# Modulation on TensorE, more work put beside choosing, more row buffers, and top sums sought among 70 pairs

## The reference, cut to what matters

```python
s_top, i_top = lax.top_k(scores, 16)            # twice 16 of 128, for two halves of a query
cand = s_top[:, :, 0, :, None] + s_top[:, :, 1, None, :]      # 16 x 16 sums
best, pos = lax.top_k(cand.reshape(..., 256), 16)
idx = i_top0[pos // 16] * 128 + i_top1[pos % 16]              # one of 16384 experts
gate = softmax(best)
h = gelu(sum_d u[idx, d] * x[d])
out = sum_k gate_k * h_k * v[idx_k]
```

```python
mod = silu(c) @ w_ada + b_ada      # 1024 x 6144; shift, scale and gate, twice each
h = rms_norm(x, g_mix) * (1.0 + scale1) + shift1
```

## Time and profile before

| | us |
|---|---|
| median of 3 runs | 3753.48 (3752.86 to 3761.49) |
| the profiled execution | 3752.87 |
| its span in the trace | 3750.8 |
| layer 1, first choice to first second product | 735.9 to 1542.5 |
| layer 2, the same | 2525.9 to 3215 |

### The profile page before, as it was taken

One profiled execution on the slowest core, in us unless ns is written; L12 is line 12 of the kernel. 1 busy time (PEld: TensorE's weight loads), 2 busy tenths in 40 slices (PEclk: granted clock), 3 DMA queues, 4 the chain that ended last, 5 costly groups with the idle time before them and its releaser, 6 DMA issues.

```text
span 3750.8 us, 46474 instructions
## 1 busy us (share of the span) xinstructions
PE 3396.3 (91%) x18582; PEld 2973.6 (79%) x18582; DVE 2809.2 (75%) x4525; ACT 1410.3 (38%) x1889; POOL 1151.4 (31%) x726
## 2 busy tenths in 40 slices
PE   6999998977777889999999899788888999999998
PEld 5978578877776879878888776778888999888887
DVE  3356543399888999578888586548999998688887
ACT  4324532232222556333333344423322566333333
POOL 0000000058788873233333000000433333233332
PEclk9999998988888999999999899889999999999999
DMA  3212133257777989999998320124777999999996
GB/s 124 79 35 68 45 103 100 79 187 249 244 249 249 305 296 363 340 341 357 362 357 330 93 68 6 68 74 140 255 249 240 311 366 354 356 361 357 363 362 238
DMA packets 373498, 855.56 MB, mean 228 GB/s; under 512 B 22449, under 2 KB 237329, under 8 KB 340130
## 3 DMA queue, kind: packets, MB, share of 16 engines
q1 hardware_dynamic: 299554, 584.12, 44.6%
q0 software_dynamic: 73728, 268.47, 20.0%
HBM read 746.58 MB, written 105.93 MB: 227 GB/s over the span
## 4 chain that ended last, share of the span: by engine, by line
PE 61%; DVE 29%; DMA 4%; ACT 3%; issue 2%; POOL 2%; SPq 0%; DVEq 0%; POOLq 0%; ACTq 0%
PE ps L294 31%; PE ps L1404 27%; DVE parts L277 6%; DVE scr L1609 5%; DMA scr<-in_p_rows_u,cst 3%; DVE scr L1652 2%; DVE scr L1586 2%; DVE scr L1590 1%; DVE scr L1584 1%; PE ps L316 1%; DVE scr L1588 1%; DVE scr L1558 1%; DVE scr L1644 1%; DVE scr L1552 1%; DVE scr L1582 1%
## 5 line engine op out<-in xcount | busy, mean ns | idle before, releaser
L294 PE MATMUL ps<-ht_hi,parts 128*128 128x384 f32 (+1 forms) x5008 | 1423.3, 360 | 98.0 <-DVE parts L277 93.7
L294 PEld LDWEIGHTS ps<-ht_hi,parts 128*128 128x128 f32 x5008 | 961.3, 197 | 158.4 <-DVE parts L277 105.3
L277 DVE TENSOR_TENSOR parts<-ring,parts 128x2048 fp32r<-128x2048 f32 (+1 forms) x317 | 740.8, 2337 | 322.8 <-ACT parts L269 322.6
L269 ACT ACTIVATE parts<-ring 128x2048 fp32r<-128x2048 f32 (+1 forms) x317 | 606.5, 1913 | 822.9 <-PE ps L1404 675.7
L294 PE MATMUL ps<-ht_lo,parts 128*128 128x384 f32 (+1 forms) x2504 | 892.5, 356 | 0.0
L322 ACT ACTIVATE scr<-ps 128x384 f32<-128x384 f32 (+3 forms) x496 | 244.1, 505 | 1131.9 <-PE ps L294 1071.5
L1737 POOL DMA_INDIRECT scr<-in_p_rows_u,cst x256 | 439.5, 1717 | 658.0 <-DVE scr L1609 471.1
L1737 POOL DMA_INDIRECT scr<-in_peer_v,cst x256 | 381.9, 1492 | 702.8 <-DVE xres L1626 609.0
L1404 PE MATMUL ps<-parts,ht_lo 128*128 128x512 f32 x2304 | 528.9, 390 | 7.2 <-DVE ht_lo L1699 7.2
L1404 PE MATMUL ps<-parts,ht_hi 128*128 128x512 f32 x2304 | 529.3, 390 | 4.5 <-DVE ht_hi L1699 4.5
L1404 PEld LDWEIGHTS ps<-parts,ht_lo 128*128 128x128 f32 x2304 | 433.6, 188 | 97.5 <-DVE ht_lo L1699 7.6
(11 more groups left out here) (227 smaller groups left out, 3013.4 us busy)
## 6 DMA issues: line engine op xcount, KB each, us to landing
ring<-in_peer_u SPq DMA_DIRECT2D x128, 1024.0 KB, 6.7
ring<-in_peer_v SPq DMA_DIRECT2D x128, 1024.0 KB, 7.6
hbuf<-scr SPq DMA_DIRECT2D x128, 384.0 KB, 7.6
gbuf<-scr SPq DMA_DIRECT2D x96, 512.0 KB, 8.9
scr<-gbuf SPq DMA_DIRECT2D x64, 768.0 KB, 9.4
scr<-hbuf SPq DMA_DIRECT2D x64, 768.0 KB, 12.1
ring<-in_w_in SPq DMA_DIRECT2D x35, 1024.0 KB, 5.3
scr<-in_w_ada SPq DMA_DIRECT2D x48, 512.0 KB, 7.6
```

What stands on the lines that cost most here:

```text
L269: e.activation(halves(m)[0], slot_view(m)[:, 0:units[m][0]], ACT.Copy).then_inc(A.sem, A.up(("hi", m)))
L277: e.tensor_tensor(lo, slot_view(m)[:, 0:units[m][0]], hi.bitcast(F32), ALU.subtract).then_inc(V.sem, V.up(("lo", m), ("slot", m)))
L294: ins = e.matmul(ps, l, r, start=(i == 0), stop=(i == n - 1))
```

## The change

1. `w_ada` is taken as TensorE's stationary operand: for each of 48 steps, 8 products of [128x128] float32 weights with one column of `silu(c)`, into column `n` of one PSUM bank that is held for all 48. One addition of the bias ([128, 48]), one transpose, one copy by ScalarE and one store follow at `n` = 48, 50 and 52. POOL has no part in it any more, and the 48 closing additions, bias loads and stores are gone. Load `n + 1` of `w_ada` is issued at step `n`.
2. `peer_order` gets other costs and two rates. Now 87 half units and 92 dots stand before the first spread step (13 half units in block 0, then 24, 25, 25 half units and 30, 31, 31 dots per block), 41 half units and 36 dots after it; the last 6 half units follow the last step.
3. `UR` has four buffers in layer 1 (the fourth where POOL's products stood) and five in layer 2.
4. The 16 largest of 16x16 sums of two sorted lists are sought among 70 pairs: place 0 with 16, places 1 to 4 with 8 each, places 5 to 15 with 2 each. Three additions make them instead of one; `top16` runs over 70 instead of 256; `places` works the pair of places out of a position in 12 operations on 128x128 float32, in place of a shift, a mask and two casts.

```diff
+        mw = [at_(MO + 1024 * k, 1024).rearrange("p (c n) -> p c n", c=NC) for k in range(2)]
+        bd, md = at_(MO + 3072, 48), at_(MO + 3136, 48)
+        mrows = at_(MO + 3200, 128)
         ct = at_(26624, 8)
-        mw = [at_(MO + 1024 * k, 1024).rearrange("p (c n) -> p c n", c=NC) for k in range(2)]
-        tm = at_(MO + 2048, 1024).rearrange("p (c n) -> p c n", c=NC)
-        bd = [at_(MO + 3072 + 128 * k, 128) for k in range(4)]
-        md, sums = [[at_(MO + 3584 + 256 * j + 128 * k, 128) for k in range(2)] for j in range(2)]
+        MOD_STEPS = 48
...
         def mod_fetch(e, w, s):
-            if s >= 48:
-                return
-            cols = slice(128 * s, 128 * s + 128)
             k = s % 2
             if s >= 2:
-                w.wait_ge(*at_point("mod_weighted", s - 2))
-            e.dma_start(mw[k], inp["w_ada_2"].rearrange("o (c p) n -> p (o c) n", p=128)[:, :, cols]).then_inc(
+                w.wait_ge(*at_point("mod_used", s - 2))
+            e.dma_start(mw[k], inp["w_ada_2"].rearrange("o (c p) n -> p (o c) n", p=128)[:, :, 128 * s:128 * s + 128]).then_inc(
                 dm_mw[k].sem, dm_mw[k].up(("ada", s), by=16))
-            if s >= 4:
-                w.wait_ge(*at_point("mod_done", s - 4))
-            e.dma_start(bd[s % 4][0:1, :], inp["b_ada_2"][:, cols]).then_inc(
-                dm_mb[s % 4].sem, dm_mb[s % 4].up(("ada_bias", s), by=16))
...
         def mod_sp(e, w, n):
             if n == 0:
                 w.wait_ge(*at_point("joined", NB - 1))
                 sp_small(e, "c_landed", ct, inp["c_2"])
+                sp_small(e, "ada_bias", bd, inp["b_ada_2"])
                 mod_fetch(e, w, 0)
-                mod_fetch(e, w, 1)
-            if n >= 2:
-                mod_store(e, w, n - 2)
-            if n >= 1:
+            if n + 1 < MOD_STEPS:
                 mod_fetch(e, w, n + 1)
-            if n == 48:
-                mod_store(e, w, 47)
+            if n == MOD_STEPS + 4:
+                w.wait_ge(*at_point("mod_rows"))
+                sp_small(e, "mod", mod_d.rearrange("(s n) -> s n", n=128), mrows[0:48, :])
...
+            if n == MOD_STEPS + 2:
+                put_act(e, w, ("modt",), mrows[0:48, :], psum(("modt",))[0:48, 0:128], ("mod_rows",))
         def mod_pe(e, w, n):
-            if n >= 1:
-                s = n - 1
-                if s >= 1:
-                    held.discard(bank_of["mod", s - 1])
-                w.wait_ge(*at_point("mod_summed", s))
-                ps = bank(w, ("mod", s))
-                matmuls(e, ps[0:1, 0:128], [(one, sums[s % 2])], ("ps", ("mod", s)))
-                held.add(bank_of["mod", s])
-            if n == 48:
-                held.discard(bank_of["mod", 47])
-        def mod_close(e, w, s):
-            w.wait_ge(*at_point("ps", ("mod", s)))
-            w.wait_ge(*at_point("ada_bias", s))
-            if s >= 2:
-                w.wait_ge(*at_point("mod_stored", s - 2))
-            e.tensor_tensor(md[s % 2][0:1, :], psum(("mod", s))[0:1, 0:128], bd[s % 4][0:1, :], ALU.add).then_inc(
-                V.sem, V.up(("free", ("mod", s)), ("mod_done", s)))
+            if n == 0:
+                w.wait_ge(*at_point("c_act"))
+                bank(w, ("mods",))
+                held.add(bank_of["mods",])
+            if n < MOD_STEPS:
+                w.wait_ge(*at_point("ada", n))
+                names = [("ps", ("mods",))] if n == MOD_STEPS - 1 else []
+                matmuls(e, psum(("mods",))[:, n:n + 1], [(mw[n % 2][:, cc, :], ct[:, cc:cc + 1]) for cc in range(NC)],
+                        ("mod_used", n), *names)
+            if n == MOD_STEPS:
+                held.discard(bank_of["mods",])
+            if n == MOD_STEPS + 2:
+                w.wait_ge(*at_point("mod_done"))
+                ps = bank(w, ("modt",))
+                e.transpose(ps[0:48, 0:128], md, ident).then_inc(P.sem, P.up(("ps", ("modt",))))
...
         def mod_dve(e, w, n):
-            if n >= 2:
-                mod_close(e, w, n - 2)
-            if n == 48:
-                mod_close(e, w, 47)
-        def mod_pool(e, w, n):
-            if n >= 48:
-                return
-            k = n % 2
-            w.wait_ge(*at_point("c_act"))
-            w.wait_ge(*at_point("ada", n))
-            if n:
-                w.wait_ge(*at_point("mod_summed", n - 1))
-            e.tensor_tensor(tm, mw[k], bc(ct.unsqueeze(2), [128, NC, 128]), ALU.mult).then_inc(
-                G.sem, G.up(("mod_weighted", n)))
-            for m in (4, 2):
-                w.wait_ge(*G.now())
-                e.tensor_tensor(tm[:, 0:m, :], tm[:, 0:m, :], tm[:, m:2 * m, :], ALU.add).then_inc(G.sem, G.up())
-            w.wait_ge(*G.now())
-            if n >= 2:
-                w.wait_ge(*at_point("ps", ("mod", n - 2)))
-            e.tensor_tensor(sums[k], tm[:, 0, :], tm[:, 1, :], ALU.add).then_inc(G.sem, G.up(("mod_summed", n)))
+            if n == MOD_STEPS:
+                w.wait_ge(*at_point("ps", ("mods",)))
+                w.wait_ge(*at_point("ada_bias"))
+                e.tensor_tensor(md, psum(("mods",))[:, 0:48], bd, ALU.add).then_inc(
+                    V.sem, V.up(("free", ("mods",)), ("mod_done",)))
...
-            costs = [3.0] * 5 + [2.5] + [2.7] * 5 + [3.0, 4.4, 3.0, 4.4, 8.0]
-            one_step, one_dot = 2.7, 1.4
-            rest = (NB - 1) * sum(costs) + STEPS * one_step
-            pace = (sum(costs) + rest + SLOTS * one_dot) / LAST
-            each = rest / (SLOTS - 4)
+            costs = [3.0] * 5 + [2.0] + [1.6] * 5 + [5.4, 4.4, 2.4, 4.4, 8.0]
+            one_step, one_dot, early = 1.65, 1.4, 92
+            pace = (NB * sum(costs) + STEPS * one_step + SLOTS * one_dot) / LAST
+            while_choosing = early / ((NB - 1) * sum(costs))
+            while_spreading = (SLOTS - early) / ((STEPS - 2) * one_step)
             def due(cost, late):
                 nonlocal at_u, slot, owed, debt
                 owed += cost
                 if chosen:
-                    debt += cost
+                    debt += cost * (while_spreading if late else while_choosing)
                 while True:
-                    if debt >= each and slot < SLOTS:
-                        debt -= each
+                    if debt >= 1 and slot < SLOTS:
+                        debt -= 1
...
-                self.UR = [at_(x, D) for x in (8192, 9216, 21504)]
+                self.UR = [at_(x, D) for x in (8192, 9216, 21504, 24576, 25600)[0:4 if nq == 16 else 5]]
...
-                    e.tensor_tensor(self.CA, bc(Tv[:, :, 0, :].unsqueeze(3), [128, 8, 16, 16]),
-                                    bc(Tv[:, :, 1, :].unsqueeze(2), [128, 8, 16, 16]), ALU.add).then_inc(V.sem, V.up())
+                    for a, na, nb, o in ((0, 1, 16, 0), (1, 4, 8, 16), (5, 11, 2, 48)):
+                        e.tensor_tensor(self.CA[:, :, o:o + na * nb].rearrange("p h (a b) -> p h a b", a=na),
+                                        bc(Tv[:, :, 0, a:a + na].unsqueeze(3), [128, 8, na, nb]),
+                                        bc(Tv[:, :, 1, 0:nb].unsqueeze(2), [128, 8, na, nb]), ALU.add).then_inc(V.sem, V.up())
...
-                    BPf = self.BP.rearrange("p h k -> p (h k)")
-                    e.tensor_scalar(self.HL[0].bitcast(U32), BPf, 4, None, ALU.logical_shift_right)
-                    e.tensor_scalar(self.HL[1].bitcast(U32), BPf, 15, None, ALU.bitwise_and).then_inc(V.sem, V.up())
+                    self.places(e, w)
                 if i in (11, 13):
                     r = (i - 11) // 2
                     it16 = c("iota")[:, 0:16]
-                    w.wait_ge(*V.now())
-                    e.tensor_copy(self.HF[r], self.HL[r].bitcast(U32)).then_inc(V.sem, V.up())
...
+            def places(self, e, w):
+                P0, A0, A1, S1 = self.PD
+                a, b = self.HF
+                e.tensor_copy(P0, self.BP.rearrange("p h k -> p (h k)")).then_inc(V.sem, V.up())
+                w.wait_ge(*V.now())
+                e.tensor_scalar(A0, P0, 0.125, -1.4375, ALU.mult, ALU.add)
+                e.tensor_scalar(A1, P0, 0.5, -19.25, ALU.mult, ALU.add).then_inc(V.sem, V.up())
+                w.wait_ge(*V.now())
+                e.tensor_scalar(A0, A0, MAGIC, None, ALU.add)
+                e.tensor_scalar(A1, A1, MAGIC, None, ALU.add).then_inc(V.sem, V.up())
+                w.wait_ge(*V.now())
+                e.scalar_tensor_tensor(out=A0, in0=A0, scalar=MAGIC, in1=A1, op0=ALU.max, op1=ALU.max).then_inc(V.sem, V.up())
+                w.wait_ge(*V.now())
+                e.tensor_scalar(a, A0, MAGIC, None, ALU.subtract).then_inc(V.sem, V.up())
+                w.wait_ge(*V.now())
+                e.tensor_scalar(A0, a, 8.0, 8.0, ALU.mult, ALU.add)
+                e.tensor_scalar(A1, a, 2.0, 38.0, ALU.mult, ALU.add).then_inc(V.sem, V.up())
+                w.wait_ge(*V.now())
+                e.scalar_tensor_tensor(out=S1, in0=a, scalar=16.0, in1=A0, op0=ALU.mult, op1=ALU.min).then_inc(V.sem, V.up())
```

(15 more changed lines are left out.)

20 lines of the change are left out of this document (8 added, 12 removed).

## The result

The kernel after takes 3662.35 us (median of 4 runs, 3659.61 to 3667.88), the kernel before 3753.77 us beside it: a ratio of 0.9754, 95% interval 0.9737 to 0.9771. That is 91 us less, inside the range, but 41 us short of the forecast of 3621 us and outside the forecast's own bounds of 3590 to 3650. The profiled execution, the slowest of the four, took 3667.9 us, with a span of 3666.1, so what is added up from its trace lies some 5 us above the median.

A forecast was written before the change was run, and what follows sets the result against it. VectorE bounds choosing and TensorE spreading, with POOL's sums holding up layer 1. Layer 2 saves 35 us and layer 1 96.6, so 3752.9 - 131.7 = 3621 us; own bounds 3590 to 3650, range 3565 to 3690.

The forecast's parts named there:

- rival D: Both layers: the new list brings nothing, only modulation and pairs pay; 3659 us, layer 2 above 665 us; chance 0.1.
- Prices of the work: Both layers: a modulation step 1.76 us of TensorE, 84 us in all; pairs save 7.6 us of VectorE per block.
- Stretched splits: Layer 1's blocks: VectorE's splits, 2911 ns while POOL computes, would take 2.29 us as in layer 2.
- and the 7 us that it waits today = 115 us: Layer 2's later blocks: VectorE 108.3 us plus today's waits bounds each, TensorE 105 us; three blocks 345 us.
- Load n + 1 is issued ... 4 half units (17 us) before it is needed: Modulation in layer 1: loads of `w_ada` land in 7.6 us, so TensorE's wait should not show except at the first step.
- step 0: First modulation step, layer 1's block 0: wait of nothing to 15 us, covered by VectorE's work, taken as nothing.
- Row buffers "at nothing": Choosing: more row buffers carry the denser dots and hide a wait of 4.5 us per block, counted at nothing.
- Spreading, 241 and 243 us: Spreading in layers 2 and 1: VectorE bounds up to the last step, then TensorE does 7 half units, 30 us.
- A: Modulation on TensorE: one-column products start 0.056 us apart, VectorE bounds layer 1 too; about 3576 us; chance 0.12.
- C: Layer 1's choosing: TensorE falls to its lower clock level, 368 us more; 3989 us, slower; chance 0.03.
- B: Both layers: DMA engines become the bound, 56 us more, 3677 us; sign, such waits over 20 us a layer; chance 0.2.

The follow-up runs named there:

- mod_only: The kernel before with only the modulation moved to TensorE; list, row buffers and 256 sums as before: 3684.87 us, ratio 0.9813.
- pairs_only: The kernel before with only the search among 70 pairs: 3729.27 us, ratio 0.9937.
- the measured weights: The kernel after with the order list's costs set near the times in its trace, the part before the turn 2.5 instead of 8.0: 3635.72 us, ratio 0.9685.
- ada_early: The kernel after with SP's load of `w_ada` put ahead of the load of the unit instead of behind it: 3645.04 us, ratio 0.9703.
- real_ada_five: The kernel after with list costs as measured, the earlier load of `w_ada` and five row buffers in layer 1 too: 3620.95 us, ratio 0.9639.
- old_list: The kernel after with the order list of the kernel before; modulation on TensorE, 70 pairs and row buffers stay: 3637.62 us, ratio 0.9688.

## Why the prediction was right, and where it was not

The sign was right, for the reasons given in most steps, and the time lay in the stated range. But that range was drawn to take in the rivals, and the time is not the forecast's 3621 us: it is the 3659 us of rival D, within 4 us. The prices of the work held; what failed is a step mis-sized, the waits and TensorE's share in layer 2's blocks, and two counted at nothing, the loads of `w_ada` and the row buffers.

- **Prices of the work: right.** A step was put at 1.76 us and takes 1.70. The Trainium skill ("TensorE: Matmul & The Clock Gate", LDWEIGHTS) has about 107 ns per load of 128 columns, which these 0.106 us bear out; the 25 ns between starts of the section "Wait — 56ns, not 53.3ns?" does not decide here. The pairs were put at 7.6 us of VectorE a block and save 7.1. VectorE in layer 2's blocks: forecast 3 x 108.3 = 324.9 us, measured 325.0.
- **Stretched splits: right.** They are gone with POOL's arithmetic (2286 ns in `mod_only`, 2696 in `pairs_only`, in layer 1's blocks), as the section on who interferes with whom of the Trainium skill's "SBUF — State Buffer" has it for two SBUF inputs against GpSimd's reads.
- **Layer 2's blocks, "and the 7 us that it waits today = 115 us": the failed step.** VectorE waits 14.2 us a block, not 7, so the three take 367.7 us, not 345. The forecast had TensorE at 105 and VectorE at 108 us a block and let the longer one decide. TensorE's share was too small: it counted half units alone, and the earlier trace rows already had 273.58/3 = 91.2 us for 20 half units of 4.26, 6 us a block more. Measured are 108.9 us a block, as much as VectorE's 108.3. Two engines so nearly even, which meet at every split and turn, wait for each other in turn; how long depends on the order: of the 22.7 us the measured weights take 14.6 back, with the engines as even as before (322.6 and 324.7 us).
- **"Load n + 1 is issued ... 4 half units (17 us) before it is needed": failed.** The step looked at the buffer's release and not at the queue. SP holds the load back behind a unit's, and where the trace was read above it leads by some 10 us. With step 0, bounded at 0 to 15 us and taken as nothing (8.8 us), this is the 17 us of `ada_early`: without it block 0 of layer 1 takes 78.4 us (forecast 80, after 87.6) and its blocks 384.6 (forecast 387, after 399.6). About half of it came by waits, and about half by busy time at a lower granted clock. The cover named for step 0, VectorE's work in block 0, was no cover: TensorE is busy 79 of 88 us there.
- **Row buffers "at nothing": failed as a price.** With the new list they hide 35 us. It spoiled the sum little, since the kernel after has them; what waits for rows are left (14.5 and 8.8 us in the blocks) were not in it as such.
- **Spreading, 241 and 243 us: right** (237.7 and 244.2). Up to TensorE's last spread step in layer 2, 204 us (forecast 203), VectorE is busy 195.1 us and TensorE 190.6, so the bound passes back to VectorE as described, by a little; then 33.7 us where 38 were forecast.
- **The rivals.** A falls by the 0.106 us, C by granted clocks of 0.97 and 0.95 in the blocks, though a step at the lower level does cost what C took, 3.40 us. B's sign, over 20 us of waits for `w_ada` or rows in a layer, came only if the two are added (13.6 + 14.5 in layer 1), and from SP's order and the number of buffers, not from the transfers' rate: `real_ada_five` moves more GB/s and waits less. D's sign came (layer 2 above 665 us: 677.3), and so did its time, 3659 us for a measured 3662. Its premise, that the list brings nothing, is what the runs show; it had 0.1 and deserved more. That the sum agrees to 3 us is in part luck: D has 743 us for layer 1 and 659 for layer 2, the kernel after 731.4 and 677.3, and without the new list (`old_list`) they are 724.9 and 657.6.

What stays open is the rest of the idle time in the best kernel: in layer 2's blocks VectorE is still idle for 28 us and TensorE for 31. No order of single items was tried that would bring these down.

## What to carry to other kernels

Work moved off one engine's stretch into another's is only worth its share of the waits: where two engines are within a few per cent of each other and meet often, add their mutual waits to the longer of them (here 7 us a block more than before with the first weights, 2 with the measured ones), and weigh an order list by durations from a trace rather than by guesses. For every new transfer look at what stands ahead of it in its queue and what that waits for, not only at when its buffer comes free, and count a wait of TensorE as more than its length while the granted clock falls with it. And take each part of a change out in turn: here one part of it cost 25 us while the whole gained 91.

## What the runs showed that was not expected

A product with a single column costs 0.106 us an instruction, as one with 64 or 192 columns and new weights does (at most 0.116 and 0.11 us), yet this is cheaper than it looks: of 82 us more on TensorE only 44.5 show in layer 1 of `mod_only`. And with the new list one row buffer more in layer 1 and two in layer 2 are worth 35 us, beside a whole gain of 91, though a gather lands in 7.6 us and a dot is asked for only every 4 us on average: the waits stand at runs of dots, nearly half of them at the three runs of five. And late loads of 13.6 us in all cost 17 us of the median and 24 us of the layer's trace, because the granted clock fell with them.
